# A four-layer streaming trunk on one core: a new order in the first round of each MLP, and two of four weight sums moved to GpSimd

## The reference, cut to what matters

```python
for i in range(4):
    h = _rmsnorm(x, norm_mix[i])
    y = mixer(i % 3)(h)          # latent attention, gated recurrence, sliding-window attention
    x = x + y
    x = x + _squared_relu_mlp(_rmsnorm(x, norm_mlp[i]), mlp_w1[i], mlp_w2[i])
return _rmsnorm(x, norm_final)

def _squared_relu_mlp(h, w1, w2):
    return jnp.square(jax.nn.relu(h @ w1)) @ w2      # 1024 -> 4096 -> 1024, 512 tokens, float32
```

## Time and profile before

| what | value |
|---|---|
| median of the runs | 2027.0 us |
| profiled execution, whole | 2027.66 us |
| its span | 2025.8 us |
| PE busy | 2000.3 us, 99% |
| DVE busy | 1432.3 us, 71% |
| ACT busy | 1063.8 us, 53% |
| POOL busy | 247.3 us, 12% |

### The profile page before, as it was taken

One profiled execution on the slowest core, in us unless ns is written; L12 is line 12 of the kernel. 1 busy time (PEld: TensorE's weight loads), 2 busy tenths in 40 slices (PEclk: granted clock), 3 DMA queues, 4 the chain that ended last, 5 costly groups with the idle time before them and its releaser, 6 DMA issues.

```text
span 2025.8 us, 28746 instructions
## 1 busy us (share of the span) xinstructions
PE 2000.3 (99%) x11760; PEld 1748.8 (86%) x11760; DVE 1432.3 (71%) x1682; ACT 1063.8 (53%) x1508; POOL 247.3 (12%) x323
## 2 busy tenths in 40 slices
PE   9999999999999999999999999999999999999998
PEld 8888898989878789899888888898988888899897
DVE  7866865756897867567698786675787758667574
ACT  6655534625466646254456663553647646353453
POOL 7002000000200200002731200000641011000000
PEclk9999999999999999999999999999999999999999
DMA  6222324314223133241332242422422223242431
GB/s 193 61 68 78 120 64 125 113 57 143 86 81 103 64 125 115 61 148 57 119 89 70 61 138 84 125 84 83 148 76 71 59 67 122 66 146 63 125 115 42
DMA packets 152595, 193.20 MB, mean 95 GB/s; under 512 B 17712, under 2 KB 95088, under 8 KB 152464
## 3 DMA queue, kind: packets, MB, share of 16 engines
q1 hardware_dynamic: 145520, 186.04, 29.6%
q0 software_dynamic: 4544, 3.94, 0.7%
q10 hardware_dynamic: 2400, 1.38, 0.2%
HBM read 185.30 MB, written 2.10 MB: 93 GB/s over the span
## 4 chain that ended last, share of the span: by engine, by line
PE 89%; DVE 6%; POOL 2%; ACT 2%; DMA 1%; issue 1%; ACTq 0%; DVEq 0%; POOLq 0%; SPq 0%
PE psum L674 27%; PE psum L676 27%; PE psum L675 27%; DVE h_lo L1514 2%; PE psum L1113 2%; PE psum L1086 1%; DVE w_lo L1479 1%; DMA arena<-in_mlp_w 1%; PE psum L1221 1%; DVE arena_r L1675 1%; PE psum L1062 1%; PE psum L1058 1%; PE psum L1057 1%; PE psum L1063 0%; DVE arena L1611 0%
## 5 line engine op out<-in xcount | busy, mean ns | idle before, releaser
L1479 DVE TENSOR_TENSOR w_lo<-w_raw,w_hi 128x1024 fp32r<-128x1024 f32 (+1 forms) x303 | 374.5, 1240 | 239.5 <-ACT w_hi L2400 238.3
L2400 ACT ACTIVATE w_hi<-w_raw 128x1024 fp32r<-128x1024 f32 (+1 forms) x307 | 323.6, 1060 | 328.3 <-PE psum L676 292.7
L674 PE MATMUL psum<-u_hi,w_hi 128*128 128x512 f32 x1256 | 492.2, 392 | 0.1
L676 PE MATMUL psum<-u_hi,w_lo 128*128 128x512 f32 x1256 | 489.1, 389 | 0.0
L675 PE MATMUL psum<-u_lo,w_hi 128*128 128x512 f32 x1256 | 489.1, 389 | 0.0
L674 PE MATMUL psum<-h_hi,w_hi 128*128 128x256 f32 (+1 forms) x1368 | 440.4, 322 | 0.0
L675 PE MATMUL psum<-h_lo,w_hi 128*128 128x256 f32 (+1 forms) x1368 | 437.5, 320 | 0.0
L676 PE MATMUL psum<-h_hi,w_lo 128*128 128x256 f32 (+1 forms) x1368 | 437.3, 320 | 0.0
L676 PEld LDWEIGHTS psum<-u_hi,w_lo 128*128 128x128 f32 x1256 | 235.8, 188 | 49.6
L674 PEld LDWEIGHTS psum<-u_hi,w_hi 128*128 128x128 f32 x1256 | 235.9, 188 | 49.0 <-DVE u_lo L1809 1.2
L674 PEld LDWEIGHTS psum<-h_hi,w_hi 128*128 128x128 f32 x1368 | 260.3, 190 | 20.2 <-issue 1.1
(11 more groups left out here) (333 smaller groups left out, 2589.3 us busy)
## 6 DMA issues: line engine op xcount, KB each, us to landing
w_raw<-in_mlp_w SPq DMA_DIRECT2D x176, 512.0 KB, 3.9
arena<-in_mlp_w SPq DMA_DIRECT2D x80, 512.0 KB, 4.9
w_raw<-in_mla_w_o SPq DMA_DIRECT2D x16, 512.0 KB, 3.8
w_raw<-in_lru_w_in SPq DMA_DIRECT2D x16, 512.0 KB, 3.9
w_raw<-in_swa_w_in SPq DMA_DIRECT2D x12, 512.0 KB, 4.2
w_raw<-in_mla_w_ukv SPq DMA_DIRECT2D x8, 512.0 KB, 4.7
w_raw<-in_lru_w_out SPq DMA_DIRECT2D x8, 512.0 KB, 3.6
w_raw<-in_swa_w_o SPq DMA_DIRECT2D x8, 512.0 KB, 4.0
```

What stands on the lines that cost most here:

```text
L674: nc.tensor.matmul(out, stat[0], mov[0], start=start, stop=False, skip_group_check=skip)
L676: return nc.tensor.matmul(out, stat[1], mov[0], start=False, stop=stop, skip_group_check=skip)
L1479: ins = nc.vector.tensor_tensor(w_lo[:, to], tile, exact(w_hi[:, to]), ALU.subtract)
L2400: nc.scalar.activation(w_hi[:, to], raw_tile(op.raw), ACT.Copy).then_inc(w_hi_done, 1)
```

## The change

Three things are edited. First, the order in the first round of each MLP: `sums_hi` and `sums_lo` stand earlier; ACT copies c11 before it takes the norm's root and before half 1's high part; DVE's `norm_var` no longer waits for the root and stands before the low part of half 0, and split 3 stands behind that low part. Second, the sums q += e and b += a of all 28 rounds are made by POOL, in a new function `weight_sums`, and ACT waits for a new semaphore `pool_sums` before it copies those two units. Third, T4 is summed by POOL. The last diff lines put `weight_sums` before the angles in POOL's queue.

```diff
@@ weight_plan, seven()
-        ops.append(Operand("A11+A21", a, (e, q), made=sums + 1))
-        ops.append(Operand("A11+A21+A22", a, (e, q), made=sums + 2))
+        ops.append(Operand("A11+A21", a, (e,), made=sums + 1))
+        ops.append(Operand("A11+A21+A22", a, made=sums + 2))
         ops.append(Operand("A12", b))
-        ops.append(Operand("A21+A22", q, (b, a), made=sums + 3))
+        rounds.append(Round(a, q, e, b, sums + 1, len(ops)))
+        ops.append(Operand("A21+A22", q, pooled=sums + 1))
         q.freed = len(ops)
         ops.append(Operand("A22", e))
         e.freed = len(ops)
-        ops.append(Operand("A11+A12+A21+A22", b, made=sums + 4))
+        ops.append(Operand("A11+A12+A21+A22", b, pooled=sums + 2))
         a.freed = b.freed = len(ops)
-        sums += 4
+        sums += 2
@@ vector engine, split()
-                    elif op.role == "A11+A21+A22":
-                        a22, a21 = op.others
-                        nc.vector.tensor_tensor(raw_tile(a21), raw_tile(a21), raw_tile(a22), ALU.add
-                                                ).then_inc(sums_made, 1)
-                    elif op.role == "A21+A22":
-                        b, a = op.others
-                        nc.vector.tensor_tensor(raw_tile(b), raw_tile(b), raw_tile(a), ALU.add).then_inc(sums_made, 1)
@@ vector engine, norm_var() and norm_scale(): root_ready() moves from the first to the second
@@ vector engine, seven_products()
                 split(1)
-                if r % 7 == 0:
-                    nc.vector.tensor_tensor(b21, b21, b11, ALU.add).then_inc(turned_made, 1)
                 split(1)
@@ vector engine, mlp()
                 nc.vector.tensor_tensor(b11, b11, b12, ALU.subtract).then_inc(turned_made, 1)
+                sums_lo()
                 c.add("gained", 4)
...
                 turned_lo(T1, b11)
-                sums_lo()
                 turned_lo(T3, b12)
...
                 squares_of(0)
-                split(1)
+                norm_var()
                 low_of_squares(0)
-                norm_var()
+                split(1)
                 squares_of(1)
@@ scalar engine, split()
-                    if op.made is None:
+                    if op.made is not None:
+                        act.wait_ge(sums_made, op.made)
+                    elif op.pooled is not None:
+                        act.wait_ge(pool_sums, op.pooled)
+                    else:
                         act.wait_ge(w_loaded[op.raw.slot], op.raw.landed)
-                    else:
-                        act.wait_ge(sums_made, op.made)
@@ scalar engine, seven_products(), behind the c11 copy and its split(1)
                 if r % 7 == 0:
+                    norm_root(bank(3, 1))
+                    c.add("psum_done")
+                    high_of_squares(1)
+                    split(1)
                     turned_hi(T4, b21)
@@ scalar engine, mlp()
-                half_gained(n - 1, range(4 if PHASES[n - 1][0] == "mla" else 0, KC))
+                if PHASES[n - 1][0] != "mla":
+                    half_gained(n - 1, range(4))
+                    sums_hi()
+                    half_gained(n - 1, range(4, KC))
+                else:
+                    half_gained(n - 1, range(4, KC))
+                    sums_hi()
                 split(1)
                 turned_hi(T1, b11)
-                sums_hi()
...
                 relu_of(1)
-                norm_root(bank(3, 1))
-                c.add("psum_done")
-                split(1)
-                high_of_squares(1)
@@ gpsimd
+            def weight_sums(i):
+
+                for n in range(i * PER_MLP, (i + 1) * PER_MLP):
+                    r = rounds[n]
+                    pool.wait_ge(sums_made, r.first)
+                    pool.wait_ge(w_loaded[r.e.slot], r.e.landed)
+                    g.tensor_tensor(raw_tile(r.q), raw_tile(r.q), raw_tile(r.e), ALU.add).then_inc(pool_sums, 1)
+                    if n % PER_MLP == 0:
+                        pool.wait_ge(turned_made, 4 * i + 3)
+                        g.tensor_tensor(b21, b21, b11, ALU.add).then_inc(turned_made, 1)
+                    pool.wait_ge(w_ready, r.split)
+                    pool.wait_ge(sums_made, r.first + 1)
+                    g.tensor_tensor(raw_tile(r.b), raw_tile(r.b), raw_tile(r.a), ALU.add).then_inc(pool_sums, 1)
@@ gpsimd, the loop over the phases
+                if kind == "mlp":
+                    weight_sums(i)
                 if kind == "mlp" and before_rotary(n):
                     angles(1 if PHASES[n + 1][0] == "swa" else 0)
```

More of the change, by code:

```diff
@@ L145, with __init__ @@
 class Operand:
-    def __init__(self, role, raw, others=(), made=None):
-        self.role, self.raw, self.others, self.made = role, raw, others, made
+    def __init__(self, role, raw, others=(), made=None, pooled=None):
+        self.role, self.raw, self.others, self.made, self.pooled = role, raw, others, made, pooled
+class Round:
+    def __init__(self, a, q, e, b, first, split):
+        self.a, self.q, self.e, self.b, self.first, self.split = a, q, e, b, first, split
 def weight_plan():
-    raws, ops, raw_starts = [], [], []
+    raws, ops, raw_starts, rounds = [], [], [], []
     sums = 0
@@ L235, in weight_plan @@
         raw.landed = landed[raw.slot]
-    return raws, ops, raw_starts
+    return raws, ops, raw_starts, rounds
 EXTRA = 2
+PER_MLP = 2 * SLICES - 1
 LOADS = {"mla_in_tail": 2, "mla_uq": 4}
@@ L267, in trunk @@
 def trunk(nc, A):
-    raws, ops, raw_starts = weight_plan()
+    raws, ops, raw_starts, rounds = weight_plan()
     with ExitStack() as ctx:
@@ L439, in trunk @@
         w_loaded = [sem(f"w_loaded{i}") for i in range(SLOTS + EXTRA)]
-        sums_made = sem("sums_made")
+        sums_made, pool_sums = sem("sums_made"), sem("pool_sums")
         gained_done = sem("gained_done")
@@ L1486, in split @@
                     elif op.role == "A11+A21":
-                        a22, _ = op.others
+                        a22, = op.others
                         dve.wait_ge(w_loaded[a22.slot], a22.landed)
                         nc.vector.tensor_tensor(tile, tile, raw_tile(a22), ALU.add).then_inc(sums_made, 1)
-                    elif op.role == "A11+A21+A22":
-                        a22, a21 = op.others
-                        nc.vector.tensor_tensor(raw_tile(a21), raw_tile(a21), raw_tile(a22), ALU.add
-                                                ).then_inc(sums_made, 1)
-                    elif op.role == "A21+A22":
-                        b, a = op.others
-                        nc.vector.tensor_tensor(raw_tile(b), raw_tile(b), raw_tile(a), ALU.add).then_inc(sums_made, 1)
             def sum_ready():
@@ L1545, in norm_var @@
                 sum_ready()
-                root_ready()
                 link(nc.vector.tensor_scalar(var[:, :], bank(3, 1), 1.0 / D, EPS, ALU.mult, ALU.add))
             def norm_scale():
+                root_ready()
                 link(nc.vector.reciprocal(root[:, :], root[:, :]))
@@ L1736, in mlp @@
                 squares_of(0)
+                norm_var()
+                low_of_squares(0)
                 split(1)
-                low_of_squares(0)
-                norm_var()
                 squares_of(1)
```

## The result

The changed kernel takes 2038.7 us (median of six runs, 2037.52 to 2040.01), the kernel before 2027.22 beside it (2026.01 to 2028.22): ratio 1.0055, 95% interval 1.0045 to 1.0065. It is slower by 11.5 us; the forecast was 6.8, to 2033.8, in a range of 2024.5 to 2039.0.

A forecast was written before the change was run, and what follows sets the result against it. PE bounds the kernel, busy 2000.3 of 2025.8 us. Starts -1.4, rounds +7.2 and POOL's queue +1.0 sum to +6.8 us on the profiled 2027.66: 2034.5, or 2033.8 for the median; range 2024.5 to 2039.

The forecast's parts named there:

- rival C: Everywhere: POOL's additions do not hold up DVE's plain additions; 19 us gained, 2008, or about half, 2017; chance 0.13.
- the signs named: Traces if right: 2.4 us POOL additions, twelve 0.6 us PE waits for c22's subtraction, four over 3 us at MLP starts.
- The starts of the MLPs: First round of each MLP: PE starts unit 3 0.4 to 0.5 us earlier, none in one MLP; -1.4 us together.
- no gain: Start of the MLP after the recurrence: sums_hi between the halves of the gained inputs delays split 1 by 0.4 us.
- the clock is hurt as before: MLP starts: the low PE clock after the wait for unit 3 costs the same as in the kernel before.
- A wait of 2.8 us costs 4.2 us there: First MLP's start, kernel before: PE's wait for unit 3 also brings the lower 1.2 GHz clock, 4.2 us in all.
- The rounds: Second rounds (g1) of slices 1 to 3, twelve in all: late c22 costs PE 0.6 us each, 7.2 us.
- POOL's queue: Angles start at about 962 and hold DVE in the last g1, 0.5 us in each of two MLPs: 1.0 us.
- The walk to c22: g1 of slice 1, first MLP: step-by-step delays from POOL's q += e to PE's unit 7, 0.6 us lost.
- Each 0.1 us of it counts twice: g1 rounds: the addition's length enters twice; 2.1 us gives 0.0, 2.6 gives 1.0 us a round, 0 to 12 in all.
- Rival B: Rounds have more room than the walk says; only the starts and small losses count, 2025.6 to 2030; chance 0.29.
- Rival D: Rounds: short waits or late squares spread, or the clock falls after them, 8 us more, 2042; chance 0.05.

## Why the prediction was right, and where it was off

- **Direction and cause: right.** POOL's addition of 1024 columns takes 2.40 us in the mean where it starts free (2.4 forecast), and shuts DVE out for 2.2. The kernel with writes in the sums' place shows that the hold is the cause, and rival C (no hold) is refuted. Of the signs named, the four waits of over 3 us for split 3 came and the wait for the norm's low part went; the twelve waits of 0.6 us for DVE's subtraction into c22 did not come. In their place stand twelve of 0.26 for the c11 copy and two of 0.21 for that subtraction, so the path by which the hold reaches PE in the rounds was forecast only in part.
- **"The starts of the MLPs", -1.4 us: +0.5 measured.** The chain in the first MLP was as forecast to 0.4 us: squares 0 at 213.59 (213.35), split 3 begun at 217.14 and over at 218.36 (218.1), PE at 218.50 (218.1). Up to the start of unit 3 the whole term was right: -0.7, +0.4, -0.7 and -0.5 us in the four MLPs, -1.5 together. The second is the one priced at "no gain": split 1 was late there by the sums_hi that now stands ahead of it. The step that failed is "the clock is hurt as before". Behind the start of unit 3 the MLPs lost 0.1, 0.9, 0.2 and 0.8 us, 2.0 together, because the low clock lasted about twice as long in the second and the fourth, and in the third fell where it had not before. That the third still won 0.5 us is luck: its new low clock cost 1.5 us, and 1.3 came back because PE no longer waited for c21.
- **"A wait of 2.8 us costs 4.2 us there": oversized.** The kernel before shows what the low clock cost in the end: 0.1 to 0.2 us at unit 6, as PE would have waited for c21 otherwise. The forecast does not use it, but rival C counts the clock at 0.8 us an MLP (1.4 less 0.6), and the expectations of the order alone and of T4 early in full. The kernel with T4 early, without a fall of the clock, won 15.5 us at the four starts. A slip that nothing rests on: between 199.97 and 213.07 DVE makes 11 operations of 1.135 us and one of 0.6, not 12 and one.
- **"The rounds", 7.2 us: 10.4 measured, with the 0.3 of POOL's queue below (0.86 per round, not 0.6).** The walk to c22 was good: split 2' held 1.2 us (1.15), L1690 at 309.37 (309.18), c22 over at 315.75 (315.56), PE at 315.80 (315.6). What failed is that the walk went straight to c22 and never asked when g1's c11 is due: the same delay of 1.2 us makes that copy late (303.41 to 304.01, PE starts unit 3 at 304.06). It takes 0.42 us, and since PE has then been pushed back already, c22's own part is 0.23 instead of 0.6. Behind either wait the next unit is 0.1 us late as well.
- **"Each 0.1 us of it counts twice": wrong share.** The two holds do not count alike. b += a on POOL alone costs the rounds nothing; q += e alone 7.6 us.
- **"POOL's queue", 1.0 us: 0.3.** The angles start at 967.50, 961.7 when PE's shift of 5.8 us there is taken off (962 forecast); the two last second rounds that they touch lose 0.14 each.
- **Rival B** (the rounds have room) falls with the twelve waits. **Rival D** had a true core: the clock did not fall in the rounds, but stayed low longer at two starts and fell at a third.

What the change was worth by parts: the new order wins 17.3 us at the starts beside the sums on POOL, and 15.5 without them once T4 isn't late on DVE; the sums on POOL take 17.8 there in the old order, and 10.5 in the rounds. T4 was what had to move, and the place for it was on DVE itself, three operations earlier.

## What to carry to other kernels

Before moving an elementwise operation to GpSimd to relieve VectorE, ask what VectorE does during it: here an operation with two SBUF inputs stood still for 2.2 us of a GpSimd addition of 2.40, about twice as long as VectorE needed to make the sum itself (1.14). The move can still be free if its release is tied to a point where VectorE is about to wait for someone else (here two units later: 10.4 us, from 2023.0 to 2012.6). And when a wait is removed by a new order, look up what stands behind it in the same queue: here the wait only moved from c11 to c21 until its input was made earlier too.

## What the runs showed of the hardware

- **Who asks first need not get the port first.** T4's addition asks for it in the middle of a DVE operation. In the kernel with T4 alone on POOL it got it at the end of that operation in three MLPs, and in the second MLP only after that operation and three more of DVE, when DVE turned to an operation with a PSUM input; in the kernel with b += a and T4 on POOL that happened in three MLPs of four. The first row is from the first MLP of the former kernel, the second from that of the latter (L3120 is T4):

```profile
206.11 3.24 POOL L3120 TENSOR_TENSOR u_lo_f<-u_lo_f,u_hi_f 128x1024 f32<-128x1024 f32 x1 [11.92 <-DVE u_hi_f L1752]
```

```profile
205.59 6.67 POOL L3120 TENSOR_TENSOR u_lo_f<-u_lo_f,u_hi_f 128x1024 f32<-128x1024 f32 x1 [11.71 <-DVE u_hi_f L1752]
```

  Both asked 0.23 us after DVE had begun split 2. In the changed kernel, where it asked 0.16 us after, it got the port at the end of that operation in all four MLPs. The other kernels divide in the same way: with q += e alone on POOL, with the old order and with halves it asked 0.16 us after and got the port at once each time, 16 of 16 with the changed kernel; with writes in the sums' place and with the sums of g0 it asked 0.23 us after, and in these four kernels together it came late in 6 of 16 places. What decides was not settled. It bears on the kernel with T4 alone on POOL: where T4 gets the port at once, in the first and third MLPs, PE waits 1.29 and 1.70 us for unit 3; in the first and third MLPs of the other, where it gets it late, PE waits 0 and 0.11 us there.
- **The clock does not follow the length of the wait alone.** In the fourth MLP of the kernel with T4 alone on POOL it fell after a wait of 1.85 us; with q += e and T4 on POOL it stayed at 1.00 in the first MLP after 3.40. First the former's unit 3 and the 3 us behind it, then the latter's:

```profile
1694.15 0.36 PE L698 MATMUL psum<-arena_r,w_hi 128*128 128x256 f32 x1 [1.85 <-DVE w_lo L1503]
...
1694.00:1697.00 3.00, 2.85 (x16) 2.88 (x17) 3.00 (x3) 2.97 (x4) 0.00 (x0) 0.62 0.00 0
```

```profile
218.03 0.36 PE L698 MATMUL psum<-arena_r,w_hi 128*128 128x256 f32 x1 [3.40 <-DVE w_lo L1503]
...
218.00:221.00 3.00, 2.97 (x25) 3.00 (x26) 2.15 (x2) 2.97 (x4) 0.00 (x0) 1.00 0.03 5
```

  After a wait of 1.77 us, in the kernel with T4 and the sums of g0 on POOL, it did not fall, nor after any shorter one. In the kernel before it fell after waits of 2.78, 2.75 and 2.74 us and not after the 2.73 of the third MLP. Each kernel's falls are read from one execution, and they need not be the same in another: the mean granted clock of the kernel before lies between 0.995 and 0.998 over its runs.
